# Prompt queries, keys and values ahead of the convolution; its twelve projection tiles in halves beside the prompt's attention items; three value buffers

## What is computed

```python
hc, gc, gb, cq, ckv, kpe = _split_last(a @ w_in, (512, 512, 512, 384, 256, 32))
up = jnp.concatenate([conv_prev, gc * hc], axis=1)
conv = conv_w[0] * up[:, 0:t]
for k in range(1, 3):
    conv = conv + conv_w[k] * up[:, k:k + t]
y_conv = gb * conv
ckv = _rms(ckv, kv_norm)
kpe = _rope(kpe, cos, sin)
q = (_rms(cq, q_norm) @ w_uq).reshape(b, t, 8, 96)
q_nope, q_pe = q[..., :64], _rope(q[..., 64:], cos, sin)
q_lat = jnp.einsum('bthn,rhn->bthr', q_nope, w_uk)
o_lat = attend(q_lat, q_pe, ckv, kpe)
y_att = jnp.einsum('bthr,rhv->bthv', o_lat, w_uv).reshape(b, t, 512)
y = jnp.concatenate([y_conv, y_att], axis=-1) @ w_out
```

## Time and profile before

| what | us |
|---|---|
| median of 3 runs | 1534.64 (1529.66 to 1536.36) |
| span of the profiled execution | 1544.0 |
| PE busy in it | 1487.7 (96%) |
| DVE busy | 1013.7 (66%) |
| ACT, POOL busy | 269.8 (17%), 102.7 (7%) |
| start of the item loop on PE | 213.9 |
| first product of the output projection | 322.48 |

### The profile page before, as it was taken

One profiled execution on the slowest core, in us unless ns is written; L12 is line 12 of the kernel. 1 busy time (PEld: TensorE's weight loads), 2 busy tenths in 40 slices (PEclk: granted clock), 3 DMA queues, 4 the chain that ended last, 5 costly groups with the idle time before them and its releaser, 6 DMA issues.

```text
span 1544.0 us, 18899 instructions
## 1 busy us (share of the span) xinstructions
PE 1487.7 (96%) x7084; PEld 1194.0 (77%) x7084; DVE 1013.7 (66%) x2038; ACT 269.8 (17%) x566; POOL 102.7 (7%) x114
## 2 busy tenths in 40 slices
PE   8999989799999999999999899999999999999996
PEld 6887645478888888888877778788888888888875
DVE  3363354568776676766774876877866766767845
ACT  4000034322101101001132321022001011011223
POOL 0012212500000000000100000400000000000100
PEclk9999988799999999999999999999999999999998
DMA  8305667622222222222213121122222222222201
GB/s 323 114 23 156 197 182 212 192 93 82 82 82 82 82 82 83 82 82 82 97 55 133 63 82 55 58 83 82 82 83 82 82 83 82 83 82 96 83 28 58
DMA packets 39469, 152.36 MB, mean 99 GB/s; under 512 B 6673, under 2 KB 19378, under 8 KB 26706
## 3 DMA queue, kind: packets, MB, share of 16 engines
q1 hardware_dynamic: 34258, 134.37, 25.0%
q0 software_dynamic: 5120, 16.78, 3.7%
HBM read 148.11 MB, written 3.02 MB: 98 GB/s over the span
## 4 chain that ended last, share of the span: by engine, by line
PE 91%; DVE 5%; another core or an unknown queue 2%; issue 1%; ACT 0%; DMA 0%; DVEq 0%; SPq 0%; ACTq 0%
PE psum L531 68%; PE psum L501 14%; PE psum L773 1%; PE psum L667 1%; PE psum L486 1%; PE psum L702 1%; PE psum L794 1%; PE psum L730 1%; PE psum L782 0%; PE psum L595 0%; PE psum L738 0%; DVE small L1553 0%; PE psum L652 0%; PE psum L835 0%
## 5 line engine op out<-in xcount | busy, mean ns | idle before, releaser
L531 PE MATMUL psum<-arena 128*128 128x272 f32 x2016 | 479.2, 393 | 0.0
L531 PEld LDWEIGHTS psum<-arena 128*128 128x128 f32 x2016 | 383.0, 190 | 78.7
L1161 DVE TENSOR_TENSOR arena<-psum,arena 128x272 f32<-128x272 f32 x564 | 248.7, 441 | 248.1 <-PE psum L531 225.1
L531 PE MATMUL psum<-B,ring 128*128 128x272 f32 x736 | 184.7, 393 | 4.1 <-ACT B L881 1.9
L501 PE MATMUL psum<-A,ring 128*128 128x272 f32 x672 | 161.0, 401 | 8.1 <-DMA ring<-in_weights 7.1
L531 PE MATMUL psum<-arena,ring 128*128 128x272 f32 x672 | 167.7, 392 | 0.0
L531 PEld LDWEIGHTS psum<-B,ring 128*128 128x128 f32 x736 | 139.0, 190 | 33.5 <-issue 2.5
L501 PEld LDWEIGHTS psum<-A,ring 128*128 128x128 f32 x672 | 129.8, 194 | 38.0 <-ACT A L1003 7.1
L531 PE MATMUL psum<-A,ring 128*128 128x272 f32 x608 | 152.6, 393 | 1.6 <-DVE A L1613 1.5
L531 PEld LDWEIGHTS psum<-arena,ring 128*128 128x128 f32 x672 | 127.4, 190 | 26.0
L531 PEld LDWEIGHTS psum<-A,ring 128*128 128x128 f32 x608 | 115.4, 190 | 26.0 <-DVE A L1613 2.0
(11 more groups left out here) (228 smaller groups left out, 1274.6 us busy)
## 6 DMA issues: line engine op xcount, KB each, us to landing
ring<-in_weights SPq DMA_DIRECT2D x98, 1024.0 KB, 4.8
arena<-in_keys SPq DMA_DIRECT2D x128, 144.0 KB
arena<-in_attw SPq DMA_DIRECT2D x1, 3072.0 KB, 21.0
h<-in_xT SPq DMA_DIRECT2D x4, 544.0 KB, 7.7
out_yT<-A SPq DMA_DIRECT2D x8, 272.0 KB, 2.3
arena<-in_pemb SPq DMA_DIRECT2D x2, 544.0 KB, 5.8
ring<-in_weights SPq DMA_DIRECT2D x2, 512.0 KB, 6.5
arena<-in_bias SPq DMA_DIRECT2D x1, 640.0 KB, 8.2
```

Of the source, the lines that this page charges most:

```text
L531: end = pe.matmul(bank(g, n), lhs[:, c, :], x(c), start=c == 0, stop=c == 3)
L1161: ins = dve.tensor_tensor(out, bank(g, n), more, ALU.add)
```

## The change

- PE makes only tiles 0 to 5 ahead of the loop, with the query sum behind tile 3 and the latent sum behind tile 5; query tiles, latent queries, keys, values and score pairs 0 and 1 follow at once.
- Tiles 6 to 17 become 24 halves (`conv_half`, 8 matmuls of 272 columns) into bank 2 or 3, one in each of steps 0 to 26 but 6, 13 and 20. DVE takes each out in the next step (`scaled_half`), and a group's convolution is cut into four parts in the steps behind.
- Turned items use bank 7 alone, the product with the values bank 6 alone.
- Score pairs 2 to 7 move into steps 0 to 5, pairs 8 to 15 into steps 12 to 20; values of g = 0 into steps 11 to 20, those of g = 1 into 26 to 32. The turned scores lie in two buffers.
- Three value buffers: one in the arena and ring slots 2 and 3. Gather s waits for value pair s-3. Units 3 to 8 use ring slots 0 and 1 alone (`ring_of`), each issued by SP behind halves that free its slot.
- K lies in `h`; SP loads x again (`x_again`) when the scores of its heads are done.
- The first halves of products P1, P3, P2 and P6 of the output projection's first group stand in steps 32, 33 and behind the loop.

```diff
@@
-T_COL = [0, 1, 3, 4, 5, 6, 7, 10, 11, 21, 22, 23, 24, 25, 26, 27, 28, 29]
-T_NQ, T_NKV = 8, 9
-T_UQ = 12
+T_COL = [0, 1, 3, 4, 6, 7]
+T_NQ, T_NKV = 5, 8
+T_UQ = 9
...
+HALF_AT = {q + q // 6: q for q in range(N_HALVES)}
+CONV_STEPS = {0: {7: 0, 8: 1, 9: 2, 10: 3}, 1: {14: 0, 15: 1, 16: 2, 17: 3}, 2: {21: 0, 22: 1, 23: 2, 24: 3},
+              3: {28: 0, 29: 1, 30: 2, 31: 3}}
+VALUES_AT = {12: 1, 13: 2, 15: 3, 16: 4, 17: 5, 18: 6, 20: 7}
+SCORES_AT = {12: 8, 13: 9, 14: 10, 15: 11, 16: 12, 18: 13, 19: 14, 20: 15}
...
+RING_OF = {3: 1, 4: 0, 5: 1, 6: 0, 7: 1, 8: 0}
...
-        v_slot = lambda s: s % 8 if s % 8 < 6 else s % 2
+        v_slot = lambda s: s % 3
+        v_use = lambda s: s // 3
+        v_buf = lambda i: vring if i == 0 else ring[:, 1 + i, :].rearrange("p (b n) -> p b n", b=4)
...
             for m in range(2):
-                keys(m)
-            for u in range(4, 9):
-                unit(u)
-            for m in range(2, 10):
                 keys(m)
             sp.wait_ge(dve_x, 4)
             sp.dma_start(a["ckvT"].rearrange("(k p) t -> p k t", p=P), ckv).then_inc(stored, 16)
+            sp.wait_ge(qs_ready, 1)
+            sp.dma_start(a["kpeT"], ssum[64:96, :]).then_inc(stored, 16)
+            for m in range(2, 8):
+                keys(m)
+            sp.wait_ge(half_tiled, 4)
+            unit(5)
+            keys(8)
+            keys(9)
+            sp.wait_ge(half_tiled, 8)
+            unit(6)
+            sp.wait_ge(half_tiled, 12)
+            unit(7)
+            for m in range(10, 15):
+                keys(m)
+            sp.wait_ge(half_tiled, 16)
+            unit(8)
+            keys(15)
+            sp.wait_ge(half_tiled, 20)
+            unit(U_OUTAB)
+            sp.wait_ge(sc_full, 24)
+            x_again(0)
+            x_again(1)
+            sp.wait_ge(half_tiled, 24)
+            unit(U_OUTAB + 3)
...
+            for s, tiles in ((2, T_COL[3] + 1), (1, T_COL[5] + 1), (0, T_UQ + 8)):
+                pool.wait_ge(psum_full, tiles)
+                gather(s)
+            for s in range(3, 16):
+                pool.wait_ge(v_used, s - 2)
+                gather(s)
...
+            def conv_half(q):
+                n, i = 6 + q // 2, q % 2
+                u = n // 2
+                w = ring[:, ring_of(u), :].rearrange("p (k m) -> p k m", k=KD)
+                pe.wait_ge(w_loaded[u % SLOTS], 16 * (u // SLOTS + 1))
+                if q >= 2:
+                    pe.wait_ge(half_free, q - 1)
+                for k in range(KD):
+                    last = pe.matmul(psum[:, 2 + i, 0:TH], w[:, k, (n % 2) * P:(n % 2 + 1) * P],
+                                     A[:, k, TH * i:TH * i + TH], start=k == 0, stop=k == KD - 1)
+                last.then_inc(half_tiled, 1)
...
                 paged(n)
+                if n in HALF_AT:
+                    conv_half(HALF_AT[n])
+                if n == 32:
+                    pe.wait_ge(w_loaded[U_OUTAB % SLOTS], 16 * (U_OUTAB // SLOTS + 1))
+                    pe.wait_ge(conv_done, 1)
+                    pe.wait_ge(pexp, 31)
+                    out_first(P1, range(2))
+                elif n == 33:
+                    pe.wait_ge(wsum_ready, 1)
+                    pe.wait_ge(pexp, 32)
+                    out_first(P3, range(2))
...
+            def scaled_half(q):
+                n, half = q // 2, (N1, N2)[q % 2]
+                dve.wait_ge(half_tiled, q + 1)
+                dve.tensor_tensor(stg[:, n % 4, half], psum[:, 2 + q % 2, 0:TH], rstd[:, half], ALU.mult).then_inc(half_free, 1)
...
+                if n in STEP_AT:
+                    conv(*STEP_AT[n])
+                if n - 1 in HALF_AT:
+                    scaled_half(HALF_AT[n - 1])
...
```

More of the change, by code:

```diff
@@ L72 @@
 NPR = H * 4
+N_HALVES = 24
+HALF_AT = {q + q // 6: q for q in range(N_HALVES)}
[3 more added lines that the diff above has]
+SCORES_AT = {12: 8, 13: 9, 14: 10, 15: 11, 16: 12, 18: 13, 19: 14, 20: 15}
+STEP_AT = {n: (c, part) for c, steps in CONV_STEPS.items() for n, part in steps.items()}
 def item(n):
@@ L261, in build @@
         k_loaded = [sem(f"k_loaded{i}") for i in range(4)]
-        v_loaded = [sem(f"v_loaded{i}") for i in range(6)]
+        v_loaded = [sem(f"v_loaded{i}") for i in range(3)]
         vidx_step = sem("vidx_step")
@@ L632, in _ @@
             ones_tile(T_N0, [ssum[:, :]])
-            for n in range(2, 7):
-                in_ab(n)
+            in_ab(2)
+            in_ab(3)
+            pe.wait_ge(act_x, 3)
+            ones_tile(T_NQ, [qsq[:, i, :] for i in range(3)])
+            in_ab(4)
+            in_ab(5)
             pe.wait_ge(act_x, 5)
-            ones_tile(T_NQ, [qsq[:, i, :] for i in range(3)])
             ones_tile(T_NKV, [qsq[:, i, :] for i in range(3, 5)])
-            in_ab(7)
-            in_ab(8)
             pe.wait_ge(attw_loaded, 16)
@@ L701, in values_pair @@
                     for bb in range(4):
-                        last = pe.matmul(psum[32 * bb:32 * bb + 32, 5, 0:R], PTs[:, 2 * r + t, 32 * bb:32 * bb + 32],
+                        last = pe.matmul(psum[32 * bb:32 * bb + 32, 5, 0:R], PTs(2 * r + t)[:, 32 * bb:32 * bb + 32],
                                          v_buf(v_slot(s))[:, bb, R * t:R * t + R], start=r == 0 and t == 0, stop=False)
@@ L707, in values_new @@
                 for bb in range(4):
-                    last = pe.matmul(psum[32 * bb:32 * bb + 32, 5, 0:R], PTs[0:32, 16, 32 * bb:32 * bb + 32],
+                    last = pe.matmul(psum[32 * bb:32 * bb + 32, 5, 0:R], PTn[:, 32 * bb:32 * bb + 32],
                                      ckv_tok, start=False, stop=True)
@@ L793, in _ @@
                             v_cols = slice((hd - 1 + odd) * VD, (hd + odd) * VD)
-                            last = pe.matmul(psum[64 * odd:64 * odd + 64, 6 + q % 2, 0:P], vtok[:, j, v_cols],
+                            last = pe.matmul(psum[64 * odd:64 * odd + 64, 6, 0:P], vtok[:, j, v_cols],
                                              PTp[:, odd, j * P:(j + 1) * P], start=j == 0, stop=j == i)
                     last.then_inc(y_full, 1)
+            pe.wait_ge(half_free, N_HALVES)
+            out_first(P2, range(2))
+            out_first(P6, range(2))
             pe.wait_ge(ol_ready, 2)
@@ L804, in _ @@
             last.then_inc(sy_full, 1)
+            pe.wait_ge(y_free, NPR // 2)
+            out_first(P1, range(2, 4))
+            out_first(P2, range(2, 4))
             pe.wait_ge(sy_ready, 1)
-            pe.wait_ge(y_free, NPR // 2)
-            for j in range(4):
+            out_first(P3, range(2, 4))
+            out_first(P6, range(2, 4))
+            product(0, P5, wsum(0, 1), lambda c: XT_AB(0, c), None, None)
+            product(0, P7, wsum(0, 3), lambda c: XT_AB(2, c), None, None)
+            product(0, P4, quarter(U_OUTAB, 1, 1), lambda c: XT_AB(3, c), None, None)
+            for j in range(1, 4):
                 group(G_OUTAB + j, B, XT_AB, (None, None), None, lambda c, n: None, lambda c: c + 1)
@@ L1068, in _ @@
                         act.wait_ge(y_full, m // 2)
-                    act.activation(PTp[:, m % 2, 0:(i + 1) * P], psum[:, 2 + m % 2, 0:(i + 1) * P], ACT.Copy)\
+                    act.activation(PTp[:, m % 2, 0:(i + 1) * P], psum[:, 7, 0:(i + 1) * P], ACT.Copy)\
                        .then_inc(pt_ready, 1)
@@ L1440, in paged @@
             def paged(n):
-                if n < 16 and n % 4 == 3:
-                    raw_max(1, n // 4)
-                elif n == 16:
+                if n in (2, 4, 6):
+                    raw_max(0, n // 2)
+                elif n == 7:
+                    soft_max(0)
+                elif n in (9, 10):
+                    turned(0, 2 * n - 18)
+                    turned(0, 2 * n - 17)
+                elif n == 11:
+                    turned(0, 4)
+                    inverse(0)
+                elif n in (14, 16, 19, 21):
+                    raw_max(1, (14, 16, 19, 21).index(n))
+                elif n == 22:
@@ L1513, in _ @@
             dve.nop().then_inc(psum_free, 1)
+            for c in range(4):
+                full(T_UK + c)
+                link(dve.tensor_copy(K[0:64, 2 * c, :], slot(T_UK + c)[0:64, 0, :]))
+                link(dve.tensor_copy(K[0:64, 2 * c + 1, :], slot(T_UK + c)[64:128, 0, :]))
+                dve.nop().then_inc(psum_free, 1)
             link(dve.tensor_copy(knew[0:96, 0, :], ckv[0:96, 0, TP:T]))
```

275 lines of the change are left out of this document (153 added, 122 removed).

## The result

On the chip on which both were timed, the changed kernel takes **1541.49 us** (median of 5, 1540.36 to 1545.12) and the kernel before 1535.04 us (5 runs, 1529.66 to 1536.36): a ratio of 1.006, 95% interval 1.0046 to 1.0074. It is 6.5 us slower. The forecast was 1518 us and faster; the time lies just inside its range of 1503 to 1542.

What follows compares the result with a forecast made beforehand. PE bounds until 190 us, then idles or slows. Front 107.6, loop work 160.7 plus waits 9.4 gives 277.7; the gather-paced tail ends at 310.2, worth 306.5: 16 us off 1544.0, less 9.4, is 1518 us; range 1503 to 1542.

Steps and rivals of the forecast that it cites:

- The base: Whole kernel: profiled execution 9.4 us above the timed median before, the same distance expected after, so 1528 profiled gives 1518 us.
- these can't be saved twice: Caveat on the 9.4 us: part may be stalls that the profile itself makes; allowed for in the range only.
- The path: First stage up to the output product: an end worth 306.5 us instead of 322.5, 16 us less.
- Front: Work ahead of the item loop: ends at 107.6 us against 213.9, norms uncovered at no cost, up to 4 us more.
- Keys: Loop step 14: key pair 10, whose DMAs stand on SP behind unit 7, comes late; a wait of 3 us.
- Turned scores: Steps 11 and 26: values follow the last turn at once and wait for DVE, 1.2 us each, 2.4 in all.
- DMA and stalls in the loop: Steps 12 to 20's transfers and the gathers' stalls: between 0 and 25 us, taken as 4.
- Tail: Behind step 26: gathers 11 to 15 take POOL 25 us from 274.0, landing 3; last value pair starts at 302.0.
- Behind: Output projection: halves of its products done early save 8 x 0.46 = 3.7 us of later work.
- The stalls follow the gathers: Rival, item loop: 13 gathers at 1.9 us each cost 25 us instead of 4; 1539, middle 1529 us; chance 0.18.
- Gathers hold PE: Rival, item loop: gathers hold PE itself, halves included, by 3.5 us; loop pays 45 instead of 4, 1559 us; chance 0.11.
- The clock: Rival, item loop: granted clock averages 0.88 again, so 160.7 us of work take 22 more; 1540 us; chance 0.09.

Runs made afterwards that it cites:

- before_third: Kernel before, no edit, on a chip that takes it in about 1535 us; 1533.4 us, span 1532.8.
- after_again: Changed kernel, no edit, timed again on a chip that takes the kernel before in 1550.06 us; 1536.66 us, ratio 0.992.
- before_again: Kernel before, no edit, profiled again; 1547.31 us against 1547.01 for the kernel before beside it.
- before_one: Kernel before with one indirect DMA of values per pair instead of four; 1521.2 us, ratio 0.9815; on another chip 1521.61 us, 0.9813.
- places_keys: Changed kernel with gathers 11 to 13 in free places right behind gather 10, and key pairs 10 and 11 ahead of unit 7; 1535.78 us, ratio 0.9931.
- half_rows: places_keys with half-length rows in every gather: same 64 indirect DMAs, 128 KB each instead of 256 KB; 1537.02 us, ratio 0.9895.
- spread: places_keys with gathers 11 to 13 held until the halves of steps 21, 23 and 25 are through; 1523.21 us, ratio 0.9838; later 0.9849 and 0.9823.
- after: Changed kernel as first timed and profiled against the kernel before; 1541.49 us, ratio 1.006.
- before_early: Kernel before with gathers 10 to 13 issued ahead of gathers 8 and 9; 1541.26 us, ratio 1.0049.

## Why the prediction was wrong, point by point

**The base, wrong: the first of two causes.** The step was "I expect the same distance" of 9.4 us between profile and median. The execution shown (span 1544.0) has the 18.7 and 11.6 us of unnamed waits of the earlier trace rows; the kernel before on a chip like the timed one (before_third) has none, and its output product starts at 310.57 us, where my path for the changed kernel had 310.2. The distance was therefore no constant of profiling (the changed kernel's own is 1543.3 - 1541.49 = 1.8 us) but the very stalls that the halves were to cover. The prediction named this ("these can't be saved twice") and gave it a place in the range only. On before_third's base (span 1532.8) the same path gives 310.2 + 1218.3 = 1528.5 us, a gain of 0.3%, within what can be told. So the base takes 11.2 of the 16 us, and the path below 15.3 more: 16 - 11.2 - 15.3 = -10.5 us between the profiled executions (-6.5 between the medians; the changed kernel's profile is the slowest of its five runs). On the second kind of chip, where profile and timing agree, the forecast difference was 16 us and 13.4 were measured, in part by luck: both ends of the stage lie 5 us later than my figures (315.7 for 310.2, 327.6 for 322.5). That 1541.49 falls inside the range is luck too: its upper end allowed for held signals and a slow clock in the loop, and neither occurred in this execution.

**The path, the second cause: 15.3 us too short** (1528 forecast for the profiled execution, 1543.3 measured), term by term:

- *Front:* 107.6 forecast, 110.8 measured. The query tiles start at 59.87 for 58.9: the norms are hidden as forecast. The query tiles take 0.6 us more than summed. The other 1.6 us are the clock: the latents' small products took 7.42 us and the two windows behind 80 us have 0.75 and 0.73, as the clock fell while the latents ran instead of behind them. From the latents' start to the loop are 28.1 us, where the sum without the clock has 24.2. On the second kind, at 0.88 and 0.95, it is 25.3, and the loop starts at 107.5. Mis-sized: 2.3 us taken, 3.9 on this chip.
- *Keys:* the mechanism right, pair 10 in step 14 behind unit 7, the size not: 8.6 us instead of 3. I took 4.6 us to issue eight keys; SP's sixteen took 8.66, and they were only asked for at 186.9, so eight keys issued by about 191 us were used at 199.5: landing took some 8 us, not 2.3 to 4.8.
- *Turned scores:* 1.37 and 1.30 us for 1.2 each. Right.
- *DMA and stalls in the loop, 4 us:* none in this execution. The work is 0.9 us less than summed, though key pair 10 and the half behind it ran at a lowered clock (2.79 and 5.07 us for 1.48 and 3.93). With that, 3.2 + 5.6 + 0.3 - 4 - 0.9 gives the end of step 26 at 281.9 instead of 277.7.
- *Tail:* mechanism right: pairs of values at POOL's pace, gather 11 released by value pair 8, five gathers in a row. Sizes: POOL 26.3 us for 25; landing 8.1 us for 3, beside units 10 and 11, whose effect on it I had given no price; POOL's start 4.5 us later, mostly by the 4.2 above. So the last pair stands at 312.9 instead of 302.0. From there to the second halves 12.0 us instead of 8.2: PE is busy all that time, but at a granted clock of 0.68. The landing was taken from the median of weights and outputs, and the nearest rows for a gather behind nineteen other issues weren't in the profile of before: its last pair had already waited long for other things.
- *Behind:* the halves done early were worth 3.2 us, forecast 3.7; 2.0 between after_again and before_again, 3.9 against before_third. Right, to about a microsecond.

**What the change did on the first kind of chip** follows from before_third: the last gather's last issue ends at 292.0 before and at 304.8 after, 12.8 us later, because three buffers release gather 11 at the end of the loop where six let POOL issue from 250 us on. The last pair of values starts 11.2 us later, the output product 14.4, and 3.9 come back behind. PE's idle time that the halves fill was no longer on the path: the gathers were. This is read from two traces; no run on this kind gives the changed kernel its buffers back.

**The rivals.** *The stalls follow the gathers*: true as a mechanism on the second kind (before_one takes away every unnamed wait and 28.9 us). Its condition, that a dense PE isn't held, is true for issues in fours: in after_again PE is busy 41.00 of the 41 us from 199 to 240, with sixteen issues in them. It is false for sixteen in a row: in places_keys and half_rows the halves themselves come in pieces. *Gathers hold PE*, slower: right in sign, wrong in cause: there was no hold at all where it was slower. *The clock*: 0.97 over the loop, no. The rule of the Trainium skill ("TensorE: Matmul & The Clock Gate", "A second HAM failure mode: psum-queue depth-cycling"), by which short stops between groups bring the clock down, did not bear on this loop. The clock did cost in front and tail, where I had priced it too low or not at all.

**Left open.** Why PE's matmuls and signals are held on some chips while POOL issues, and not on others; what the changed kernel takes on the first kind with units 10 and 11 held until the last gather has landed; and what spread takes there. That the profile shown came from a chip of the second kind is argued from its waits and its time, not shown.

## What to carry to other kernels

When a profiled execution is further above the timed median than its kind usually is, find out in which stage the difference lies before you spend that stage's idle time: the same stall can't be both profile's and yours. Idle time beside indirect DMAs is to be priced by what the last of them needs: its issues, its landing, and the weights that SP issues beside it. Before you fill waits with work, see whether the buffers still let POOL start early; here that was worth as much (argued from the traces). And on chips of the second kind gathers are best issued four or eight at a time with pauses between, beside dense work on PE: spread did that and took some 0.9% off places_keys, and stands 1.5 to 1.8% below the kernel before.

## What the runs showed of the hardware

- The same kernel takes 1533 to 1536 us on two chips and in the first comparison, and 1547 to 1552 us on four chips, which is more than the change is worth, and the sign of the change goes with it (1.006 and 0.992).
- On the second kind, signals of PE to ACT and DVE are late by up to 13 to 14 us (idle time 18.0 and 16.5) while POOL issues sixteen indirect DMAs back to back (0.95 us each with 0.30 between), and arrive 3 us behind the last issue; PE's own matmuls come in pieces. Halving the bytes leaves it as it is (15.3 and 16.8 us of idle). On the first kind 24 issues without a pause, 261.9 to 292.0 us in before_third, hold nobody.
- A gather's landing, from its last issue to its pair of values, took 2.5 to 2.9 us with no weight unit issued beside it, 5.0 to 5.7 with one, and 8.1, 9.7 and 9.9 with two to four (after, before_third, before_early). The last three are all of the first kind, where SP has the units early enough. The Trainium skill ("DMA: Bandwidth & Descriptors", "Anatomy of one DMA — SWDGE (gpsimd) path") puts one such DMA at about 2 us and its bytes; the 2.5 to 2.9 us agree, those with units beside them don't.
